# A two-network kernel: the first up block of the second network multiplied before its norm factor is known

## The reference, cut to what matters

```python
x = x + gate * (merged @ w_out_2)                 # modulated residual, gate from c
h = rmsnorm_2(x, norm2_g_2) * (1 + scale) + shift # scale and shift per feature, from c
up = h @ w_up_2                                   # 1024 -> 2 * 2816: a gate half and a value half
up = causal_dwconv(up, ffn_conv_w_2, ffn_conv_b_2)# three taps over the positions
x = x + gate2 * ((silu(up_gate) * up_value) @ w_down_2)
```

## Time and profile before

| what | value |
|---|---|
| median of three runs | 1548.7 us (1546.91 to 1548.97) |
| the profiled execution | 1547.28 us, span of its instructions 1545.5 us |
| mean granted TensorE clock | 0.986 of full |
| TensorE busy | 1496.3 us, 97% |
| VectorE, ScalarE, GpSimd busy | 798.0, 577.6, 657.1 us |
| low parts of weights on GpSimd (L650) | 239, mean 2397 ns |
| high parts of weights on ScalarE (L765) | 239, mean 1031 ns |
| loads of up blocks | 44, 512 KB each, median 3.8 us from issue to landing |

### The profile page before, as it was taken

One profiled execution on the slowest core, in us unless ns is written; L12 is line 12 of the kernel. 1 busy time (PEld: TensorE's weight loads), 2 busy tenths in 40 slices (PEclk: granted clock), 3 DMA queues, 4 the chain that ended last, 5 costly groups with the idle time before them and its releaser, 6 DMA issues.

```text
span 1545.5 us, 21719 instructions
## 1 busy us (share of the span) xinstructions
PE 1496.3 (97%) x7323; PEld 1191.8 (77%) x7323; DVE 798.0 (52%) x1258; ACT 577.6 (37%) x949; POOL 657.1 (43%) x314
## 2 busy tenths in 40 slices
PE   8999999999999999999999899998999999999997
PEld 7768668788888888887767687665887888888886
DVE  5382384652443435764994505564546565654121
ACT  5412573432313224323972325553224232222222
POOL 5333454444444444434334345352543444444442
PEclk9999999999999999999999999999999999999998
DMA  5434211455545555423333134110332333333332
GB/s 154 136 110 117 82 56 55 137 162 164 169 146 176 155 177 157 123 70 93 91 90 85 58 103 76 35 41 14 97 96 71 100 99 95 95 95 91 98 89 90
DMA packets 285176, 160.25 MB, mean 104 GB/s; under 512 B 44930, under 2 KB 272770, under 8 KB 285114
## 3 DMA queue, kind: packets, MB, share of 16 engines
q1 hardware_dynamic: 283566, 156.31, 35.2%
q10 hardware_dynamic: 1548, 3.15, 0.6%
HBM read 156.78 MB, written 5.80 MB: 105 GB/s over the span
## 4 chain that ended last, share of the span: by engine, by line
PE 47%; issue 35%; POOL 12%; DVE 3%; ACT 2%; DMA 1%; POOLq 0%; SPq 0%; ACTq 0%; DVEq 0%
PE ps L1983 13%; PE ps L1985 13%; PE ps L1984 13%; POOL WL L650 11%; PE ps L2466 2%; PE ps L2477 1%; PE ps L2490 1%; PE ps L2219 1%; PE ps L2279 1%; PE ps L2336 1%; PE ps L2293 1%; DVE UL L1664 0%; DMA Wraw<-in_w_in 0%; DVE actL L1609 0%; ACT LP L941 0%
## 5 line engine op out<-in xcount | busy, mean ns | idle before, releaser
L650 POOL TENSOR_TENSOR WL<-Wraw,WH 128x1024 fp32r<-128x1024 f32 (+2 forms) x239 | 572.7, 2397 | 804.0 <-ACT WH L765 804.0
L765 ACT ACTIVATE WH<-Wraw 128x1024 fp32r<-128x1024 f32 (+2 forms) x239 | 246.3, 1031 | 741.6 <-PE ps L1985 716.8
L1983 PE MATMUL ps<-actH,WH 128*128 128x512 f32 x1256 | 502.8, 400 | 11.7 <-POOL WL L650 6.4
L1985 PE MATMUL ps<-actH,WL 128*128 128x512 f32 x1256 | 491.6, 391 | 0.0
L1984 PE MATMUL ps<-actL,WH 128*128 128x512 f32 x1256 | 491.4, 391 | 0.0
L1983 PEld LDWEIGHTS ps<-actH,WH 128*128 128x128 f32 x1256 | 237.4, 189 | 77.3 <-issue 13.8
L1985 PEld LDWEIGHTS ps<-actH,WL 128*128 128x128 f32 x1256 | 237.2, 189 | 50.6
L1984 PEld LDWEIGHTS ps<-actL,WH 128*128 128x128 f32 x1256 | 237.5, 189 | 50.1 <-issue 2.9
L1983 PE MATMUL ps<-UH,WH 128*128 128x512 f32 x576 | 228.0, 396 | 7.8 <-DVE T L1837 4.1
L1985 PE MATMUL ps<-UH,WL 128*128 128x512 f32 x576 | 225.4, 391 | 0.0
L1984 PE MATMUL ps<-UL,WH 128*128 128x512 f32 x576 | 225.3, 391 | 0.0
(11 more groups left out here) (276 smaller groups left out, 1474.4 us busy)
## 6 DMA issues: line engine op xcount, KB each, us to landing
Wraw<-in_w_ff SPq DMA_DIRECT2D x64, 512.0 KB, 4.1
Wraw<-in_w_in SPq DMA_DIRECT2D x56, 512.0 KB, 4.0
wada<-in_w_ada SPq DMA_DIRECT2D x64, 384.0 KB, 4.4
Wraw<-in_w_up SPq DMA_DIRECT2D x44, 512.0 KB, 3.8
Wraw<-in_w_down SPq DMA_DIRECT2D x16, 448.0 KB, 3.7
Wraw<-in_w_proj_rnn SPq DMA_DIRECT2D x16, 320.0 KB, 3.1
Wraw<-in_w_proj_mla SPq DMA_DIRECT2D x8, 512.0 KB, 3.9
Wraw<-in_w_out SPq DMA_DIRECT2D x8, 512.0 KB, 3.8
```

The source lines that it names most:

```text
L650: nc.gpsimd.tensor_tensor(WL[slot][:, 0:kts, :], Wraw[slot][:, 0:kts, :], WH[slot][:, 0:kts, :].bitcast(F32), ALU.subtract).then_inc(s_lo, 1)
L765: A(WH[slot][:, 0:kts, :], Wraw[slot][:, 0:kts, :], ACT.Copy).then_inc(s_hi, 1)
L1983: MM(o, wh, ah, start=first, stop=False)
L1985: return MM(o, wl, ah, start=False, stop=last)
```

## The change

Block 0 of gUp is multiplied in its raw form. ScalarE makes x * gain in high precision right after each tile's square (`raw_high`, into unused tiles of UH) and VectorE its low part (`raw_low`, into UL), while the output phase runs. Block 0's product goes to PSUM bank 6 (`raw_product`), started before the factor is known; the spread stands between its tiles 1 and 2. The shift's share of block 0 is one column, made by eight matmuls of the unsplit weights by the shift vector (`raw_columns`, bank 3), between the first and the second sum. Afterwards VectorE multiplies bank 6 by the factor (`raw_scale`), and ScalarE adds the column and writes bank 6 again (`raw_shift`); block 0's convolution reads that.

The filler matmuls are gone from this place. The pair with staggered tiles is now blocks 1 and 2, RAW_LAG = 6 tiles apart; block 3 follows by itself and waits for up_value 1. On ScalarE the high part of block 1 comes before the last square, that of block 2 between the tiles 3 and 4 of `norm_highs`, that of block 3 ahead of `raw_shift`. On GpSimd the low part of block 1 comes before the power instead of behind it. SyncE's queue loads block 2 only after the column is made. VectorE's and ScalarE's first rounds of gUp are written out of their loops.

```diff
@@ SyncE
-            stream(gUp, 2, FT, ...)
+            stream(gUp, 2, 1, cols(ups, KT, lambda i, j: D_FF2 * j))
+            sp.wait_ge(*R_("summed", "n5", 1))
+            stream(gUp, 2, FT - 1, ..., first=2)
@@ GpSimd
             low(gUp.n0, gUp.slot(0))
+            low(gUp.n0 + 1, gUp.slot(1))
             power("n5")
-            low(gUp.n0 + 1, gUp.slot(1))
@@ ScalarE
+            def raw_high(name, k):
+                A(raw_tile(UH, name, k), xT[:, ds(k, 1), :]..., ACT.Copy, scale=raw_gain(name, k)
+                  ).then_inc(R_("high", name, 0)[0], 1)
+            def raw_shift(name, bank):
+                col = shc[:, RAW[name][0]:RAW[name][0] + 1]
+                act.wait_ge(*R_("summed", name, 1))
+                own.done(A(col, ps[:, bank, 0:1], ACT.Copy))
+                act.wait_ge(*R_("scaled", name, 1))
+                A(ps[:, 6, :], T[0][:], ACT.Identity, bias=col).then_inc(R_("shifted", name, 0)[0], 1)
...
+                        if last and j == 1:
+                            next_high(1)
                         square(name, 2 * i + j, j, (s_ev, 2 * i + (ph.b0 + j + 1)))
-                    if last:
-                        next_high(1)
+                        raw_high(name, 2 * i + j)
...
+            def up_high2(k):
+                if k == 4:
+                    high(gUp, 2, gUp.n0 + 2, landed(gUp, 2))
+            norm_highs("n5", KT, ..., up_high2)
+            high(gUp, 3, gUp.n0 + 3, landed(gUp, 3))
+            raw_shift("n5", 3)
@@ VectorE
+            def raw_low(name, k):
+                dve.wait_ge(*R_("high", name, k + 1))
+                V.scalar_tensor_tensor(raw_tile(UL, name, k), xT[:, ds(k, 1), :]..., raw_gain(name, k),
+                                       raw_tile(UH, name, k).bitcast(F32), ALU.mult, ALU.subtract
+                                       ).then_inc(R_("low", name, 0)[0], 1)
+            def raw_scale(name, ph, by):
+                dve.wait_ge(s_mm, ph.n0 + 1)
+                V.tensor_tensor(T[0][:], ps[:, 6, :], by, ALU.mult).then_inc(R_("scaled", name, 0)[0], 1)
+                dve.wait_ge(*R_("shifted", name, 1))
...
+            adds(gOut2, "n5", 2 * KT, raw="n5")(KT // 2 - 1)
+            raw_low("n5", KT - 1)
             dve.wait_ge(s_ev, gOut2.b0 + KT)
             mean("n5")
             norm_parts("n5", KT, ...)
+            own.done(V.tensor_copy(rstd[:], ps[:, 2, :]))
+            raw_scale("n5", gUp, rstd[:])
@@ TensorE
+            def raw_columns(name, ph, shift, bank):
+                pe.wait_ge(s_lo, ph.n0 + 1)
+                for k in range(KT):
+                    mm = MM(ps[:, bank, 0:1], Wraw[ph.slot(0)][:, k, :], mod[:, shift + k:shift + k + 1],
+                            start=(k == 0), stop=(k == KT - 1))
+                mm.then_inc(R_("summed", name, 0)[0], 1)
+            def raw_product(name, ph, between):
+                pe.wait_ge(s_lo, ph.n0 + 1)
+                for k in range(KT):
+                    between(k)
+                    pe.wait_ge(*R_("low", name, k + 1))
+                    mm = three(ps[:, 6, :], ..., raw_tile(UH, name, k), raw_tile(UL, name, k), k == 0, k == KT - 1)
+                mm.then_inc(s_mm, 1)
...
-            norm_factors("n5")
+            sum_first("n5")
+            pe.wait_ge(S("mod_ready"), 2)
+            raw_columns("n5", gUp, 3 * KT, 3)
+            sum_last("n5")
+            def n5_spread(k):
+                if k == 2:
+                    spread("n5", N("n5", "power", 1))
+            raw_product("n5", gUp, n5_spread)
...
-            pair_product(gUp, gUp.n0, x_in, lambda k: N("n5", "low", k + 1), lambda j: [(s_ev, gOut2.b0 + KT - 1 + j)],
-                         lag=LAG)
-            repeat(pe, FT - 1, lambda p: up_round(p + 1))
+            pair_product(gUp, gUp.n0 + 1, x_in, lambda k: N("n5", "low", k + 1), lambda j: [(s_ev, gOut2.b0 + KT - j)],
+                         lag=RAW_LAG, first=1)
+            block_product(gUp, gUp.n0 + 3, 1, 0, x_in, 0, None, [(S("up_value"), 1)])
+            repeat(pe, FT - 2, lambda p: up_round(p + 2))
```

More of the change, by code:

```diff
@@ L242, in hybrid_stack @@
         gainA = keep("gainA", [P, 2, KT])
+        shc = keep("shc", [P, 2])
         nsp = keep("nsp", [P, 3, RT])
@@ L414, in N, with raw_tile, raw_gain, R_ @@
                           "summed": 1 if running else tiles, "done": tiles * (1 - split)}.get(kind, tiles * split)
+        RAW = {"n5": (1, FT - KT)}
+        RAW_LAG = 6
+        def raw_tile(u, name, k):
+            return u[:, ds(k + RAW[name][1], 1), :].rearrange("p a t -> p (a t)")
+        def raw_gain(name, k):
+            return gainA[:, RAW[name][0], ds(k, 1)]
+        def R_(kind, name, v):
+            nth = list(RAW).index(name)
+            return S("raw_" + kind), v + nth * (KT if kind in ("high", "low") else 1)
         FF_SLOTS = 2 * KT
@@ L1268, in up_round @@
                     for h in range(2):
-                        sem, v = landed(gUp, 2 * j + 2 + h)
-                        high(gUp, h, 4 * p + (gUp.n0 + 2 * j + 2 + h), (sem, 32 * p + v))
+                        if j or not isinstance(p, int):
+                            sem, v = landed(gUp, 2 * j + 2 + h)
+                            high(gUp, h, 4 * p + (gUp.n0 + 2 * j + 2 + h), (sem, 32 * p + v))
                     up_parts(2 * p + j, j)
@@ L1335, in add_square, with adds @@
                 V.tensor_tensor(T[acc][:], T[acc][:], T[at + j][:], ALU.add).then_inc(N(name, "added", 0)[0], 1)
-            def adds(ph, name, gate=None, per=1):
+            def adds(ph, name, gate=None, per=1, raw=None):
                 def body(i):
@@ L1348, in body @@
                         add_square(name, 2 * i + j, j)
+                        if raw is not None and (j or not isinstance(i, int) or i):
+                            raw_low(raw, 2 * i + (j - 1))
                 return body
@@ L2067, in norm_factors, with pair_product @@
                 keep_clock(7)
-            def pair_product(ph, n, actin, ready, evac, order=range(KT), lag=KT, between=None):
+            def raw_columns(name, ph, shift, bank):
[5 more added lines that the diff above has]
+            def raw_product(name, ph, between):
+                slot = ph.slot(0)
+                pe.wait_ge(s_lo, ph.n0 + 1)
+                for k in range(KT):
+                    between(k)
+                    pe.wait_ge(*R_("low", name, k + 1))
+                    mm = three(ps[:, 6, :], WH[slot][:, k, :], WL[slot][:, k, :], raw_tile(UH, name, k), raw_tile(UL, name, k),
+                               k == 0, k == KT - 1)
+                mm.then_inc(s_mm, 1)
+            def pair_product(ph, n, actin, ready, evac, order=range(KT), lag=KT, between=None, first=0):
                 for step in range(KT + lag):
@@ L2084, in pair_product @@
                             pe.wait_ge(*ready(k))
-                        mm = three(ps[:, ph.bank(j), :], WH[ph.slot(j)][:, k, :], WL[ph.slot(j)][:, k, :], actin(0, k),
+                        mm = three(ps[:, ph.bank(first + j), :], WH[ph.slot(first + j)][:, k, :], WL[ph.slot(first + j)][:, k, :], actin(0, k),
                                    actin(1, k), at == 0, at == KT - 1)
```

34 lines of the change are left out of this document (21 added, 13 removed).

## The result

| | before | after |
|---|---|---|
| median of 20 executions each | 1548.84 us (1545.73 to 1553.26) | 1554.64 us (1551.91 to 1558.5) |
| ratio, 95% interval | | 1.0034 [1.0025, 1.0043] |
| the profiled execution | 1547.28 us | 1556.85 us |
| its span, granted clock | 1545.5 us, 0.986 | 1555.1 us, 0.980 |

The change costs 5.3 us by the ratio and 5.8 by the medians. The forecast was 1.5. Two executions of the kernel before, of 1994.76 and 3836.53 us, fell in a slow state and count in no median and no ratio here. The first lines to set beside those of before are TensorE's busy time and, of the same page, the groups of matmuls that read UH and UL.

What follows compares the result with a forecast made beforehand. TensorE, busy 97% of the span, was the bound. 5.44 us of product fills the gap and pacing partly goes, but 0.95 + 0.85 + 1.65 and 3.0 us come: +1.5, 1548.8 (1550.2 against the median), range 1546.9 to 1553.1.

Steps and rivals of the forecast that it cites:

- rival (a): Seam and block 3: the clock falls to half at the new stall, +3.1, or +3.9 with the sums' fall; chance 0.30.
- The condition I set for block 3: Block 3's start: the clock falls if its wait reaches three us, costing 1.6 us.
- The filler goes: Between the sums and first up tiles: the 32 filler records are removed, with no cost given.
- the stretch at 648.87: Earlier 3.70 us of one-column matmuls followed by half clock; likened to the new columns, 0.8 us, +2.3 alone.
- The rest of the kernel moves along: Everything behind block 4 only shifts by block 4's delay, +1.5 us.
- Output phase: Each tile's added ScalarE copy and VectorE low part fit idle time: cost 0, at most 0.75 us once.
- the columns: Between first and second sum: eight one-column matmuls take 1.9 us and cost 0.95 on the factor's chain.
- Both meetings of GpSimd and VectorE: VectorE's low parts of raw tile 7 and normalized tile 4 wait for GpSimd's whole low part; the second costs 1.65 us.
- Block 3 waits for the value convolution: Block 3 shares block 1's bank and waits for up_value 1, behind the shift and block 0's gate convolution; 3.0 us stall.
- The chain of the factor: Sums, mean, power, spread: the spread starts 1.8 us late, half from the columns, half from GpSimd and VectorE excluding each other.
- The stall before block 3: TensorE, free at 1184.9, stands 3.0 us until block 3 starts at 1187.85.
- the +1.5 forecast: Block 4 starts at 1193.3 instead of 1191.8, so the whole kernel takes 1.5 us more.

Runs made afterwards that it cites:

- after_padded: The changed kernel with 64 unused bytes behind its shift column, so all later buffers lie at multiples of 128 bytes: 1559.49 us, 1.0069 against before.
- before_no_filler: The kernel before without its 16 filler matmuls between the sums, the power and the first tiles: 1552.24 us against 1549.99, 1.0007.
- after_unmoved: The changed kernel with its shift column in an unused half of a small buffer, so no other buffer moves: 1552.52 us against 1548.93 before, 1.0031.
- b128_spare: The kernel before with 128 unused bytes per partition behind gainA: 1557.5 us, 1.005.
- bm128_spare: The kernel before with its 128-byte buffer nsp laid behind all others, so everything behind it starts 128 bytes lower: 1557.67 us, 1.0059.
- value_first: after_padded with block 1's value convolution ahead of the wait for the shift and block 0's gate convolution: 1557.25 us against 1559.49.
- value_first_unmoved: after_unmoved with block 1's value convolution ahead of the wait for the shift and block 0's gate convolution: 1549.72 us, 1.0003 against before.
- filled_unmoved: after_unmoved with filler put back, three matmuls on each side of the columns and ten before block 3: 1554.24 us, 1.0034 against before.
- the three reordered kernels: value_first_unmoved with sums reordered among raw tiles; then columns before the spread; then also filler in block 1's waits: 1550.32, 1549.81, 1546.89 us.

## Why the prediction was wrong, point by point

- **The clock, the first step that failed.** The forecast kept the clock at full and gave a fall 0.30 as rival (a): 0.8 us at the sums, 1.6 at block 3, +3.9 with both. In the change it fell at both places. At block 3 the size was right: the block took 7.16 us instead of 5.44. At the sums it was too small by half: the first normalized tile came about 1.6 us later for it, as TensorE in tile 1 held up the spread and the spread itself went at half clock. That +3.9 lies so near the measured 3.77 is partly luck, for the queueing in it was about 1 us too high. The condition I set for block 3, a wait of three us, was too strict: the clock fell behind 2.02 us, though not each time (after_padded). Two waits of 2.98 to 2.99 us had been followed by a fall, and I made these cases a condition; they said nothing of shorter waits. "The filler goes" was priced at nothing; the likeness to the stretch at 648.87 was the right reading, and before_no_filler shows a fall at the same place. By the Trainium skill, "TensorE: Matmul & The Clock Gate", section "HAM oscillation — how this bites in real kernels", waits between groups of matmuls let the clock fall; at block 3 the trace of the change agrees (a wait of 2.02 us, then half clock), that of after_padded does not, and at the sums no wait stood ahead of the fall.
- **A term that was missing, the second step that failed.** "The rest of the kernel moves along" was wrong: new bytes in the middle of the buffers made the steps of 1728 other matmuls about 2 ns longer in the mean, 2 to 3 us. No rival had it. The falls alone would have left the time inside the stated range up to 1553.1: after_unmoved, the same seam with nothing moved, has 1552.52. With the moved buffers it is 1554.64.
- **Right.** Output phase and TensorE's order: the columns take 1.93 us (1.9 forecast). Both meetings of GpSimd and VectorE: 1.15 and 1.47 us more than 0.74 (the second forecast at 1.65). Block 3 waits for the value convolution.
- **Right in kind, off in size.** The chain of the factor queued as forecast: the power ended at t0 + 5.76, which with the clock at full has the spread at 5.8 (5.98 forecast). But the spread was 2.47 late, not 1.8: TensorE at half clock was still in tile 1 until 6.65; the spread at half clock then took 1.91 instead of 1.16, so the first normalized tile was 3.2 late. The stall before block 3 was 2.0 instead of 3.0: from block 1's end to block 3 went 6.9 us, not 7.75, as the first three convolution instructions follow each other in 2.3 us, not in 2.63 as in the earlier trace rows, and the shift came 0.3 sooner.
- **The sum.** Against block 3's start the forecast was 0.5 short, in block 3 itself 1.7 (7.16 us instead of 5.44). What queueing alone costs is known only roughly: 0.45 by the rows of the change, 1.1 to 2.3 by the times of after_unmoved, and the +1.5 forecast lies among them. Clock (2.5 by the times, 3.3 by the rows) and placement (2 to 3) make the rest of 5.3 to 5.8.

## What to carry to other kernels

Price every new wait and every removed filler twice, at full and at half clock, and don't take the higher clock for the likelier because a wait is shorter than those seen to lower it (here one of 2.0 us was followed by half clock in two profiles of three); put product, not one-column work, between the steps of a norm. A buffer added in the middle of the allocation is an edit of its own: put it at the end or in a gap, and compare the step between matmuls in a phase that was not touched. Where a chain frees a bank, do first what frees the bank, as the value convolution here (2.8 us by the medians for putting one convolution ahead of another).

## What the runs showed of the hardware that was not expected

- The step of 128x512 matmuls changes with where the moving operand (or its distance to the weights) lies: 227.2, 229.1 to 229.6, 232.7 and 227.2 ns with UH and UL moved by 0, 64, 128 and 256 bytes, and 232.7 by -128. With 128 bytes either way the whole kernel takes 7.7 to 9.1 us more of 1549 (b128_spare, bm128_spare).
- The clock fell 2.8 to 3.4 us behind t0 in all seven profiles that lack the old filler and have no product between the sums (the change, after_padded, after_unmoved, value_first, value_first_unmoved, filled_unmoved and before_no_filler); it held where two tiles of product stood between the sums (the three reordered kernels) and in the kernel before with its filler.
- A VectorE instruction with two SBUF inputs that meets one of GpSimd's ended 0.55 us behind it in both new cases, as in the earlier trace rows: it waits for the whole of it, not for a share. In the trace of before 78 of 84 such meetings end 0.53 to 0.57 us behind GpSimd's low part of the weights, the other six 0.81 to 1.17. A copy with one SBUF input can meet it too: those of 128x16 from T to gKc take 0.18 us by the median and 2.33 in a meeting.
